# Head norms whose sums take two fp32r passes, and a causal mask that is added on VectorE

## The reference

```python
def rms_norm(x, gain):
    y = x * lax.rsqrt(jnp.mean(x * x, axis=-1, keepdims=True) + EPS)
    return y * gain
# shared K, V and forget gate, from the residual stream
k = rms_norm(k.reshape(B, S, 16, 64), k_norm_gain)
f_cum = jnp.cumsum(log_sigmoid(f + forget_bias), axis=1)
# the layer's own queries
q = rms_norm(q.reshape(B, S, 16, 64), q_norm_gain)
# every block of 128 queries, every head
logits = einsum('bhqd,bkhd->bhqk', q_blk, k) * 64 ** -0.5
logits = logits + fq_blk[..., None] - fk[:, :, None, :]
logits = jnp.where(k_pos[None, :] <= q_pos[:, None], logits, -inf)
p = softmax(logits)
```

## Time and profile before

| | |
|---|---|
| Median of 3 runs | 3190.28 us (3190.12 to 3190.55) |
| The profiled execution's own time | 3188.14 us |
| Its span | 3186.6 us |
| Granted clock of PE, mean | 0.99 |
| PE (matmul) busy | 3112.2 us, 98% |
| PE weight load busy | 2490.5 us, 78% |
| VectorE (DVE) busy | 1309.2 us, 41% |
| ScalarE (ACT) busy | 860.1 us, 27% |
| GpSimd (POOL) busy | 222.6 us, 7% |

### The profile page before, as it was taken

The page is one execution under the profiler, slowest core; times in us unless marked ns, Lnnn a source line. Parts: engine busy times, 40 slices in busy tenths (PEclk is TensorE's granted clock), DMA queues, the critical chain, the costliest instruction groups (busy, mean ns, idle before and its releaser), DMA issues.

```text
span 3186.6 us, 34635 instructions
## 1 busy us (share of the span) xinstructions
PE 3112.2 (98%) x13814; PEld 2490.5 (78%) x13814; DVE 1309.2 (41%) x1427; ACT 860.1 (27%) x1025; POOL 222.6 (7%) x343
## 2 busy tenths in 40 slices
PE   5999999999999999999999999999999999999999
PEld 4788888887778888888887777766767788888887
DVE  6664233255555333333353252145444533333323
ACT  4111222222242111111134344234244311111112
POOL 0000010000010000000010011023021000000000
PEclk8999999999999999999999999999999999999999
DMA  5555565533201111111113324355241111111111
GB/s 219 198 171 202 176 226 196 180 110 105 101 27 40 53 53 42 51 53 41 52 40 106 112 83 159 101 116 125 64 109 50 40 53 53 39 53 53 39 53 53
DMA packets 144600, 302.45 MB, mean 95 GB/s; under 512 B 10193, under 2 KB 72068, under 8 KB 144516
## 3 DMA queue, kind: packets, MB, share of 16 engines
q1 hardware_dynamic: 111156, 185.90, 17.6%
q0 software_dynamic: 33360, 115.38, 11.7%
HBM read 245.93 MB, written 55.18 MB: 94 GB/s over the span
## 4 chain that ended last, share of the span: by engine, by line
PE 92%; DVE 4%; ACT 1%; DMA 1%; issue 1%; POOL 0%; SPq 0%; DVEq 0%; ACTq 0%; POOLq 0%
PE ps L1478 10%; PE ps L1479 10%; PE ps L1475 10%; PE ps L1436 8%; PE ps L1439 8%; PE ps L1442 8%; PE ps L1578 5%; PE ps L1581 5%; PE ps L1584 5%; PE ps L1841 4%; PE ps L1552 3%; PE ps L1556 3%; PE ps L1555 3%; PE ps L1699 1%; PE ps L1671 1%; PE ps L1798 1%
## 5 line engine op out<-in xcount | busy, mean ns | idle before, releaser
L1475 PE MATMUL ps<-z_hi,w_hi 128*128 128x512 f32 x1408 | 552.0, 392 | 0.0
L1479 PE MATMUL ps<-z_hi,w_lo 128*128 128x512 f32 x1408 | 547.9, 389 | 0.0
L1478 PE MATMUL ps<-z_lo,w_hi 128*128 128x512 f32 x1408 | 547.8, 389 | 0.0
L1436 PE MATMUL ps<-h_hi,w_hi 128*128 128x512 f32 x1152 | 452.2, 392 | 3.6 <-DVE w_lo L967 3.6
L1439 PE MATMUL ps<-h_lo,w_hi 128*128 128x512 f32 x1152 | 449.0, 390 | 0.0
L1113 DVE SCALAR_TENSOR_TENSOR xT<-ps,ada,xT 128x512 f32<-128x512 f32 x352 | 258.9, 750 | 442.8 <-PE ps L1479 442.8
L638 ACT ACTIVATE w_hi<-w_raw 128x2048 fp32r<-128x2048 f32 x116 | 221.4, 1909 | 743.4 <-PE ps L1475 487.7
L967 DVE TENSOR_TENSOR w_lo<-w_raw,w_hi 128x2048 fp32r<-128x2048 f32 x116 | 265.7, 2291 | 240.3 <-ACT w_hi L638 240.2
L1442 PE MATMUL ps<-h_hi,w_lo 128*128 128x512 f32 x1152 | 355.1, 389 | 0.0
L1578 PE MATMUL ps<-h_hi,w_hi 128*128 128x512 f32 x768 | 304.5, 396 | 10.1 <-DVE xT L1113 5.5
L1475 PEld LDWEIGHTS ps<-z_hi,w_hi 128*128 128x128 f32 x1408 | 264.3, 188 | 56.6 <-issue 2.2
(11 more groups left out here) (251 smaller groups left out, 3626.9 us busy)
## 6 DMA issues: line engine op xcount, KB each, us to landing
misc<-w_ada SPq DMA_DIRECT2D x80, 512.0 KB, 5.0
w_raw<-w_mlp_in SPq DMA_DIRECT2D x32, 1024.0 KB, 5.5
w_raw<-w_mlp_out SPq DMA_DIRECT2D x32, 1024.0 KB, 5.0
w_raw<-ret_w_in SPq DMA_DIRECT2D x24, 1024.0 KB, 7.4
ada_first<-w_ada SPq DMA_DIRECT2D x4, 2048.0 KB, 14.6
qk_s<-stage POOLq DMA_DIRECT2D x16, 512.0 KB, 3.5
v_s<-stage POOLq DMA_DIRECT2D x16, 512.0 KB, 3.4
g_s<-stage POOLq DMA_DIRECT2D x16, 512.0 KB, 4.2
```

What stands on the lines that cost most here:

```text
L1436: m = MM(outs[hf], hi, b_hi[:, k, cols], start=first, stop=False)
L1475: mm = MM(out_bank, hi, z_hi[:, k, half(hf)], start=k == 0, stop=False)
L1478: MM(out_bank, hi, z_lo[:, k, half(hf)], start=False, stop=False)
L1479: mm = MM(out_bank, lo, z_hi[:, k, half(hf)], start=False, stop=k == 3)
```

## The change

Three parts.

The squares of the head norms. ScalarE's square goes to `sq_high`, an fp32r tensor in the place where the fp32 squares were, so the result is rounded. GpSimd computes the same square in fp32 into `misc` slot j%2, waits for both, and puts the difference of the two into the same place as fp32r (`sq_low`). PE waits for both and multiplies `mean_head`, now fp32r, by the rounded part and by the rest, each half in turn.

GpSimd's order. Each trip, now written out and not a hardware loop, does the squares of units 0, 1 and 2, the saves of 0 and 1, the square of 3 and the saves of 2 and 3. Before the FQ bodies it waits until the ten gate DMAs have landed, because `misc` slots 0 and 1 are overwritten.

The mask. For heads 1 to 15 the score tile's last product is left out. VectorE adds a row of zeros with the causal mask at its end (`row_mask`, bf16) to the scores and takes the minimum of the negated sum, in one instruction that writes the masked scores back to PSUM. Head 0 keeps the old way.

```diff
@@ constants
-            chain(nc.vector.memset(mean_head[:], 0.0))
-            nc.vector.memset(mean_head[0:64, 0:64], 1.0 / FOX_DH)
-            nc.vector.memset(mean_head[64:128, 64:128], 1.0 / FOX_DH)
+            plain = w_raw[:, 0, 0:P]
+            chain(nc.vector.memset(plain, 0.0))
+            nc.vector.memset(plain[0:64, 0:64], 1.0 / FOX_DH)
+            nc.vector.memset(plain[64:128, 64:128], 1.0 / FOX_DH)
             chain(nc.vector.memset(mean_all[:], 1.0 / D))
+            nc.vector.tensor_copy(mean_head[:], plain).then_inc(mean_ready, 1)
@@ SyncE, before the first weight load
+            sp.wait_ge(mean_ready, 1)
@@ GpSimd
-            def spill_heads(hi_s, lo_s, u_base):
-                with pool.Fori(0, 2) as i:
-                    for j in range(4):
-                        ... (wait for the high part, save it; wait for the low part, save it)
+            def spill_heads(hi_s, lo_s, a_base, u_base):
+                def low_squares(i, j):
+                    pool.wait_ge(a_free, i * 4 + (a_base + j + 1))
+                    if i or j >= 2:
+                        pool.wait_ge(hsum_full, i * 4 + (u_base + j - 1))
+                    sq = misc[:, j % 2, :]
+                    nc.gpsimd.tensor_tensor(sq, stage[:, j, :], stage[:, j, :], ALU.mult).then_inc(hsq_step, 1)
+                    pool.wait_ge(hsq_step, i * 4 + (u_base + j + 1))
+                    pool.wait_ge(hsq_ready, i * 4 + (u_base + j + 1))
+                    nc.gpsimd.tensor_tensor(sq_low[:, j % 2, :], sq, sq_high[:, j % 2, :].bitcast(F32), ALU.subtract)\
+                        .then_inc(hsq_low_ready, 1)
+                def trip(i):
+                    low_squares(i, 0)
+                    low_squares(i, 1)
+                    low_squares(i, 2)
+                    save(i, 0)
+                    save(i, 1)
+                    low_squares(i, 3)
+                    save(i, 2)
+                    save(i, 3)
+                for i in range(2):
+                    trip(i)
+            pool.wait_ge(stat_full, 5)
@@ GpSimd, after the ten gate DMAs
-            spill_heads(fq_hi_s, fq_lo_s, 8)
+            pool.wait_ge(f_saved, 160)
+            spill_heads(fq_hi_s, fq_lo_s, A_FQ, 8)
@@ ScalarE
-                    nc.scalar.activation(stage[:, T_SLOT + j % 2, :], stage[:, j, :], ACT.Square)\
-                      .then_inc(hsq_ready, 1)
+                    nc.scalar.activation(sq_high[:, j % 2, :], stage[:, j, :], ACT.Square).then_inc(hsq_ready, 1)
@@ VectorE, row_max
-                nc.vector.tensor_reduce(neg_max[:, i:i + 1], score_pair(h, t)[:, 0:P * (i + 1)],
-                                        AX.X, ALU.max, negate=True).then_inc(s_read, 1)
+                tile, w = score_pair(h, t), P * (i + 1)
+                if h == 0:
+                    nc.vector.tensor_reduce(neg_max[:, i:i + 1], tile[:, 0:w], AX.X, ALU.max, negate=True)\
+                        .then_inc(s_read, 1)
+                else:
+                    nc.vector.tensor_tensor_reduce(out=tile[:, 0:w], in0=tile[:, 0:w], in1=row_mask[:, S - w:S],
+                                                   scale=-1.0, scalar=3e38, op0=ALU.add, op1=ALU.min,
+                                                   accum_out=neg_max[:, i:i + 1]).then_inc(s_read, 1)
@@ VectorE, once, after head 0's maxima
+            nc.vector.memset(row_mask[:, 0:S - P], 0.0).then_inc(row_mask_set, 1)
+            nc.vector.tensor_copy(row_mask[:, S - P:S], mask_b[:]).then_inc(row_mask_set, 1)
+            dve.wait_ge(row_mask_set, 2)
@@ PE, head_sums
+                pe.wait_ge(hsq_low_ready, u + (j + 1))
                 for hf in range(2):
-                    m = MM(pair[2 + j % 2][:, cols], mean_head[:], stage[:, T_SLOT + j % 2, cols], start=True, stop=True)
+                    MM(pair[2 + j % 2][:, half(hf)], mean_head[:], sq_high[:, j % 2, half(hf)], start=True, stop=False)
+                    m = MM(pair[2 + j % 2][:, half(hf)], mean_head[:], sq_low[:, j % 2, half(hf)], start=False, stop=True)
@@ PE, score_tile
-                MM(dst[:, w - P:w], ident_b[:], mask_b[:], start=False, stop=True).then_inc(s_full, 1)
+                if h == 0:
+                    m = MM(dst[:, w - P:w], ident_b[:], mask_b[:], start=False, stop=True)
+                m.then_inc(s_full, 1)
```

More of the change, by code:

```diff
@@ L118, in build @@
         xT = sb("xT", [P, KT, S])
-        ((h_hi, h_lo), (rq, rk, rv, rg, rdec, qdec, rs, k_tok, qd), (q1, k1, q2, k2, fv, fog), (out_stage,),
+        ((h_hi, h_lo), (rq, rk, rv, rg, rdec, qdec, rs, k_tok, qd), (q1, k1, q2, k2, fv, fog, row_mask), (out_stage,),
          (ada_first,)) = region(
@@ L126, in build @@
             [("q1", [P, 3, S], F32R), ("k1", [P, 3, S], F32R), ("q2", [P, 3, S], F32R), ("k2", [P, 3, S], F32R),
-             ("fv", [P, 2, 8, P], F32), ("fog", [P, S], F32)],
+             ("fv", [P, 2, 8, P], F32), ("fog", [P, S], F32), ("row_mask", [P, S], BF16)],
             [("out_stage", [P, 8, S], F32)],
@@ L130, in build @@
         (z_hi, z_lo), (stage, cosT, sinT), (_, wf_hi, wf_lo), (_, q2_first, k2_first), (
-            _, rq_first, rk_first, rv_first) = region(
+            _, rq_first, rk_first, rv_first), (_, sq_high) = region(
             32 * 1024,
@@ L137, in build @@
             [("above_ret", [P, 4, S], F32), ("rq_first", [P, 2, HALF], F32), ("rk_first", [P, 2, HALF], F32),
-             ("rv_first", [P, 4, RET_DV], F32)])
+             ("rv_first", [P, 4, RET_DV], F32)],
+            [("above_sq", [P, 4, S], F32), ("sq_high", [P, 2, S], F32R)])
         w_raw = sb("w_raw", [P, 2, 2048])
@@ L141, in build @@
         w_lo = sb("w_lo", [P, 2, 2048], F32R)
-        (misc,), (q1_first, k1_first) = region(
-            20 * 1024, [("misc", [P, 5, S], F32)], [("q1_first", [P, S], F32R), ("k1_first", [P, S], F32R)])
+        (misc,), (sq_low,), (q1_first, k1_first) = region(
+            20 * 1024, [("misc", [P, 5, S], F32)], [("sq_low", [P, 2, S], F32R)], [("q1_first", [P, S], F32R), ("k1_first", [P, S], F32R)])
         low_tiles = sb("low_tiles", [P, 2, S])
@@ L146, in build @@
         mean_all = sb("mean_all", [P, P])
-        mean_head = sb("mean_head", [P, P])
+        mean_head = sb("mean_head", [P, P], F32R)
         one_col = sb("one_col", [P, 1])
@@ L229, in build @@
         gate_k_s, gate_q_s = scratch("gate_k_s", (FOX_HEADS, 6, S)), scratch("gate_q_s", (FOX_HEADS, 4, S))
-        const_step, const_ready = sem("const_step"), sem("const_ready")
+        const_step, const_ready, mean_ready = sem("const_step"), sem("const_ready"), sem("mean_ready")
         small_loaded, pos_loaded, wf_loaded = sem("small_loaded"), sem("pos_loaded"), sem("wf_loaded")
@@ L250, in build @@
         hsq_ready, hsum_full = sem("hsq_ready"), sem("hsum_full")
+        hsq_step, hsq_low_ready = sem("hsq_step"), sem("hsq_low_ready")
         hvar_ready, hrstd_done = sem("hvar_ready"), sem("hrstd_done")
@@ L278, in build @@
         log_done, inv_done, y_read, y_gated = sem("log_done"), sem("inv_done"), sem("y_read"), sem("y_gated")
-        ones_set = sem("ones_set")
+        ones_set, row_mask_set = sem("ones_set"), sem("row_mask_set")
         out_copied, out_done = sem("out_copied"), sem("out_done")
@@ L557, in _, with save @@
             sum_squares(2)
-            def spill_heads(hi_s, lo_s, u_base):
-                with pool.Fori(0, 2) as i:
-                    for j in range(4):
[L562 to L567, removed]
+            def spill_heads(hi_s, lo_s, a_base, u_base):
[9 more added lines that the diff above has]
+                        .then_inc(hsq_low_ready, 1)
+                def save(i, j):
+                    wait_run(qk_hi_done, i * 4 + (u_base + j + 1))
+                    pool.dma_start(hi_s[bass.ds(i * 4 + j, 1)].rearrange("a p n -> p (a n)"),
+                                   qk_hi[:, j % 2, :].bitcast(F32)).then_inc(qk_hi_saved[j % 2], 16)
+                    spill(j, lo_s[bass.ds(i * 4 + j, 1)].rearrange("a p n -> p (a n)"),
+                          qk_lo_done, i * 4 + (u_base + j + 1))
+                def trip(i):
[10 more added lines that the diff above has]
+            pool.wait_ge(stat_full, 5)
+            spill_heads(fk_hi_s, fk_lo_s, A_FK, 0)
             with pool.Fori(0, 2) as i:
@@ L1761, in head_sums @@
                 for hf in range(2):
-                    cols = slice(hf * HALF, (hf + 1) * HALF)
-                    m = MM(pair[2 + j % 2][:, cols], mean_head[:], stage[:, T_SLOT + j % 2, cols], start=True, stop=True)
+                    MM(pair[2 + j % 2][:, half(hf)], mean_head[:], sq_high[:, j % 2, half(hf)], start=True, stop=False)
+                    m = MM(pair[2 + j % 2][:, half(hf)], mean_head[:], sq_low[:, j % 2, half(hf)], start=False, stop=True)
                 m.then_inc(hsum_full, 1)
+            pe.wait_ge(mean_ready, 1)
             for i in range(2):
@@ L1799, in score_tile @@
                 for c0, c1 in chunks:
```

(6 more changed lines are left out.)

## The result

The changed kernel takes 3202.49 us (median of 6 runs, 3200.11 to 3203.93), the kernel before 3190.2 beside it (6 runs): ratio 1.0038, 95% interval 1.0028 to 1.0048, or 12.1 us slower (8.9 to 15.3). The forecast was 15.2 us slower, at the upper end of that interval. The profiled execution took 3203.46 us and its span is 3201.9, 15.3 more than before.

The account below looks back on a forecast made before the run. PE, busy 98% of the span, was taken to bound the kernel. Edit 1 at +21.5 us and edit 2 at -6.3 made +15.2, forecast 3205.5 us beside 3190.28, range 3195 to 3220.

Parts of the forecast that it names:

- four last sums, without the clock: Last sum of each head-norm body: PE waits for GpSimd's product and difference, +3.5 us in each of four bodies.
- clock behind them: Behind each body's last sum: PE's pause of 5.4 us drops the granted clock, 1.7 us lost a fall.
- sums 0 and 1, three bodies: FK's two trips and FQ's trip 1: GpSimd's four instructions hidden behind unit 2, -1.62 us a body.
- sums 0 and 1 of FQ 0, with its clock: FQ's trip 0: GpSimd's squares wait for the gate DMAs, +3.9 us, and one more clock fall, 1.7.
- masks: Attention heads: 120 of 128 mask products leave PE, each holding it 0.065 us, -7.8 us.
- given back for VectorE: Attention heads: the fused maximum takes 0.06 us more an instruction, 0.1 us a head given back, 1.5 us.
- GpSimd's pair: Head norms: product and difference of 128x1024 on GpSimd, 2.4 us each, 5.0 with waits; ends 4.5 and 5.3.
- T+6.3: Last sum of a body: GpSimd done 6.3 us after T, when unit 3's last product has been issued.
- rival that the clock stays up: Head norms: clock falls depend on more than the pause, so 8.5 us go: 3197.0 us; chance 10%.
- 2.98 us record: GpSimd instruction at 947.13, normally 1.3 us, held up by VectorE; cited for the slower-GpSimd rival, 3217 to 3220, 13%.
- dear-mask rival: Attention heads: a mask costs PE more than its distance shows, -28.7 instead of -7.8 us: 3183; chance 5%.
- half-rate rival: Attention heads: VectorE's fused maximum runs at half rate, each head 3 us later, +45 us: 3250; chance 6%.

Follow-up runs that it names:

- run with filled pauses: The changed kernel with 20 more fp32r products of 128x512 on PE ahead of each body's last sum, overwritten by it; ratio 1.0005 to the kernel before.
- edit 1: The split sums of squares; its run of its own was the changed kernel with the mask products back on PE: ratio 1.0061 to the kernel before.
- both-masks run: The kernel before with the fused maximum on VectorE and all mask products still on PE, so the mask is added twice; ratio 1.0001 to the kernel before.
- edit 2: The mask change; its run of its own was the kernel before with the fused maximum and without 120 mask products: ratio 0.9976 to the kernel before.
- VectorE run: The changed kernel with FQ's first squares in other misc slots and the squares' product and difference on VectorE, not GpSimd; ratio 0.9987 to the kernel before.
- moved slots: The changed kernel with the squares of FQ trip 0's first two units in misc slots 3 and 4; ratio 1.0016 to the kernel before.

## Why the prediction was right

The sign, the bound and the place were right: PE pauses before each body's last sum, the clock falls behind it, FQ's trip 0 waits for the gate DMAs. The terms of its sum beside what was measured (us):

| term | predicted | measured | by |
|---|---|---|---|
| four last sums, without the clock | +14.0 | +10.3 | 4 x 2.57, the run with filled pauses |
| clock behind them | +6.8 | +7.8 | 1.48 + 1.95 + 2.09 + 2.28, the same run |
| sums 0 and 1, three bodies | -4.9 | -4.9 | ledger |
| sums 0 and 1 of FQ 0, with its clock | +5.6 | +4.9 | ledger |
| edit 1 | +21.5 | +18.05; +19.5 (15.3 to 23.9) | ledger; run of its own |
| masks | -7.8 | -8.2 | 120 x 0.068, both-masks run |
| given back for VectorE | +1.5 | 0 | both-masks run |
| edit 2 | -6.3 | -7.7 (-10.8 to -4.8) | run of its own |

*The last sum, sized too high.* The step that was off is GpSimd's pair: 5.0 us assumed, 4.31 measured (1.89, 0.07 between, 2.34), below my lower end of 4.5. It ends at T+5.61 and not at T+6.3. The difference was as I took it, 2.34 to 2.40 for 2.4 where nothing else ran. The product was not: it reads one tile twice and took 1.89 to 1.92 us. The Trainium skill, "GPSIMD Engine Reference", section 3.1, had led to 2.37 us as an estimate; the trace agrees for the difference and not for the product. (The "2 us lower" beside that estimate leaves out the 0.2 us of waits in a pair; with them it is 0.4 us.) A second, smaller omission: before, PE lost 0.40 us behind the fp32 sums when it went back to fp32r products (1718.21 to 1718.84, where the rest come every 0.23), and with fp32r sums it doesn't. At full clock PE's four passes were through at T+6.78 (run with filled pauses, GpSimd's end at T+5.68), predicted T+7.28: 0.5 us, which with the 0.4 makes the 0.93 us a body.

*The clock, right, and now shown.* I took 1.7 us a fall from the 2.83 us pause of FK's first product. The filled pauses show the fall to be the pause's and give 1.5 to 2.3 us a fall. The rival that the clock stays up is out: in the changed kernel's head norms all five pauses of 3.1 us and more were followed by passes at half clock. The 2.78 us pauses of the VectorE run led there too: 0.76 us for the pass right behind the pause in FQ's bodies, the fourth pass in FK 1, and a product 1.5 us behind the pause in FK 0. So shortening the pause by 40% doesn't bring the clock back; doing other work does.

*Sums 0 and 1 in trip 1, just hidden, and they were:* 12.69 for 14.33. The margin was larger than the 0.26 us that I had: GpSimd's four instructions took 10.6 us in FK 1, the weight difference's part included, and not 12.3, so they were done at 1752.14 where PE asked for sum 1 at 1753.94.

*FQ's trip 0, by the mechanism predicted, its time in part by luck.* On the time scale of the kernel before (less 4.62) the gate DMAs had landed at 1899.1, predicted 1898.5, and the next unit began at 1909.7, predicted 1909.5. That is three differences that cancel: the landing 0.5 us late, two pairs of 8.6 us and not 10.0, and sum 1's passes, which at half clock took 1.85 us instead of 0.91 and which I had counted with the clock. Moving the squares out of the way took 7.0 us off.

*Who blocks whom.* VectorE's gain at 1716.47 takes 2.35 us in place of 1.28: it stands until GpSimd's difference is through at 1717.73. I had said that it would cost PE nothing, and it doesn't: it lies beside PE's wait. What such a block costs on the path shows with the moved slots, 4.33 us for one difference, as the 2.98 us record had warned. GpSimd against VectorE alone, undisturbed, is 2.34 to 1.23 us for the difference (1.9 times) and 1.89 to 1.23 for the product (1.5), where the prediction had about twice.

*The mask, right in size.* Distance and not duration was the price: 0.068 us where the record's 0.234 is latency, so the dear-mask rival is out (it wanted 28 us). The half-rate rival is out too: 1.233 us for 1024 columns, as the plain maximum's 1.225. The fused form has a second instruction of 0.133 us that I didn't know of, 16.0 us over the kernel instead of 120 x 0.06 = 7. VectorE's gaps took it; with the masks on PE, its period is the same with it and without.

*What was not in the sum.* 4.3 us in the periods around heads 0, 1, 8 and 9, in the profiled execution: heads do grow longer in two places, 5.7 us behind head 1 and 1.8 behind head 9, though the ordinary ones shrink. Head 0's scores run against a burst of loads whose start is set elsewhere, and PE gets the maxima of head 1 only 0.4 to 0.5 us behind its last load. So PE waits as long as it is early for the burst's end. That moves from kernel to kernel (1.20, 2.70, 3.12, 3.79, 4.03 and 4.60 us before head 1 in six of them, one execution of each), so it isn't either edit's own. That the 15.3 us between the two profiles equals the forecast is luck: it had edit 1 3.5 us too high and the heads 4.4 too low, and 0.9 lies outside both stages. By the runs it is 12.1 in one measurement and 11.8 edit by edit, 3 us under the forecast. Why the wait ahead of head 9 differs (3.01 us before, 3.89 after) stays open.

## What to carry to other kernels

When work moves from the bounding engine to a slow one, ask for the place where the bounding engine has nothing else in its queue: there what the slow engine takes longer, and the clock's fall behind the pause, comes back as time. The split of the squares lost 19 us where it was put. It won 12 over plain sums in the same places once four sums stood behind other work, worth 26.5 by itself, and FQ's first squares no longer waited for the gate DMAs, worth 7. Before giving up such a change, move the consumer behind the next piece of independent work.

## What the hardware showed that I had not expected

- GpSimd's 128x1024 product of a tile with itself takes 1.89 us undisturbed, its difference of two tiles 2.34 to 2.40. No run tells the shared input from the operation and from the fp32r output.
- The fused add and minimum with a reduced output is two VectorE instructions: 1.233 us for 1024 columns, 0.311 for 128, and 0.133 more each for the readout.
- Behind plain fp32 products the first fp32r product held PE 0.63 us instead of 0.23; behind fp32r sums it did not.
- The fall of the clock can come late: behind the same 3.1 us pause in FQ's trip 0 the changed kernel's next pass was already slow, while in the run with filled pauses the four passes came at full speed and the clock was 0.59 only in the stretch behind them:

```profile
1908.00:1910.00 2.00, 0.65 (x3) 0.59 (x4) 1.57 (x1) 0.39 (x1) 2.00 (x2) 1.00 0.00 0
1910.00:1912.00 2.00, 2.00 (x7) 1.55 (x6) 0.29 (x1) 1.41 (x2) 2.00 (x1) 0.59 0.00 0
```

- The two transfers of 4 KB that bring head 1's maxima, issued by SyncE, took 6.0 us while GpSimd's burst of loads ran out and 2.5 us with the burst over. In ten kernels PE's next product came 0.4 to 0.5 us after the burst's last landing.
